# First layer's projections with both halves of h streamed past each weight, and eight modulation slabs moved into the networks

## The reference, cut to what matters

```
proj = jnp.einsum("bsd,dn->bsn", h, w_in)
q, k, v, f_logit, g_b, g_c, hc, gate_conv, gate_attn = jnp.split(proj, _SPLITS, axis=-1)
ya = g_b * causal_depthwise_conv(g_c * hc, conv_w)
yb = forgetting_attention(q, k, v, logf)
merged = sigmoid(gate_conv) * (ya @ w_branch[0]) + sigmoid(gate_attn) * (yb @ w_branch[1])
m = merged @ w_out
...
mod = c_act @ ada_w[i] + ada_b[i]      # second block, layers 0 and 1
h = rms_norm(x, norm_g[i, 0]) * (1.0 + sc_a) + sh_a
```

## Time and profile before

| | us |
|---|---|
| median of 3 runs | 962.9 (962.7 to 963.29) |
| the profiled execution | 962.54, its span 961.2 |
| TensorE busy | 953.2 (99% of the span) |
| VectorE busy | 740.0 (77%) |
| ScalarE busy | 544.8 (57%) |
| GpSimd busy | 34.2 (4%) |
| HBM read | 223.49 MB, mean 234 GB/s over the span |

### The profile page before, as it was taken

One profiled execution on the slowest core, in us unless ns is written; L12 is line 12 of the kernel. 1 busy time (PEld: TensorE's weight loads), 2 busy tenths in 40 slices (PEclk: granted clock), 3 DMA queues, 4 the chain that ended last, 5 costly groups with the idle time before them and its releaser, 6 DMA issues.

```text
span 961.2 us, 13438 instructions
## 1 busy us (share of the span) xinstructions
PE 953.2 (99%) x5418; PEld 827.7 (86%) x5418; DVE 740.0 (77%) x1145; ACT 544.8 (57%) x838; POOL 34.2 (4%) x58
## 2 busy tenths in 40 slices
PE   9999999999999999999999999999999999999997
PEld 7999989888888888888888888888888888888886
DVE  7799978788877767988678878766897678766563
ACT  6745553565455656665565454656776675454551
POOL 2000000020000001000000000001000100000000
PEclk9999999999999999999999999999999999999999
DMA  9877788498777753776467677763743266668511
GB/s 366 335 276 263 262 308 313 173 200 343 269 295 300 286 204 135 270 269 264 185 248 296 247 293 271 270 250 137 241 138 125 88 243 239 219 184 320 176 44 45
DMA packets 33151, 225.64 MB, mean 235 GB/s; under 512 B 4058, under 2 KB 4341, under 8 KB 6720
## 3 DMA queue, kind: packets, MB, share of 16 engines
q1 hardware_dynamic: 30960, 219.43, 61.8%
q0 software_dynamic: 1696, 5.08, 2.0%
q10 hardware_dynamic: 432, 0.26, 0.1%
HBM read 223.49 MB, written 1.26 MB: 234 GB/s over the span
## 4 chain that ended last, share of the span: by engine, by line
PE 93%; DVE 2%; DMA 2%; ACT 2%; SPq 0%; POOL 0%; issue 0%; DVEq 0%
PE psum L623 30%; PE psum L628 16%; PE psum L668 10%; PE psum L669 10%; PE psum L670 10%; PE psum L585 3%; PE psum L586 3%; PE psum L587 3%; DMA raw<-in_qk 2%; PE psum L888 2%; PE psum L740 1%; PE psum L739 1%; PE psum L741 1%; PE psum L320 1%; PE psum L956 1%; PE psum L601 0%
## 5 line engine op out<-in xcount | busy, mean ns | idle before, releaser
L512 DVE TENSOR_TENSOR low<-raw,high 128x2048 fp32r<-128x2048 f32 (+1 forms) x160 | 361.1, 2275 | 95.1 <-ACT high L506 95.0
L506 ACT ACTIVATE high<-raw 128x2048 fp32r<-128x2048 f32 (+1 forms) x160 | 299.9, 1897 | 15.1 <-DMA raw<-in_moba_qk 4.8
L623 PE MATMUL psum<-h_both,high 128*128 128x512 f32 x1272 | 305.3, 392 | 0.0
L623 PEld LDWEIGHTS psum<-h_both,high 128*128 128x128 f32 x1272 | 235.5, 188 | 48.2 <-issue 1.5
L628 PEld LDWEIGHTS psum<-h_both,low 128*128 128x128 f32 x1312 | 168.3, 191 | 6.4
L628 PE MATMUL psum<-h_both,low 128*128 128x256 f32 x1312 | 170.2, 283 | 0.0
L668 PE MATMUL psum<-high,y_hi 128*128 128x512 f32 x328 | 129.3, 394 | 0.0
L669 PE MATMUL psum<-low,y_hi 128*128 128x512 f32 x328 | 128.1, 391 | 0.0
L670 PE MATMUL psum<-high,y_lo 128*128 128x512 f32 x328 | 127.8, 390 | 0.0
L635 ACT ACTIVATE work_v<-psum 128x256 f32<-128x256 f32 x120 | 45.6, 383 | 142.2 <-PE psum L628 142.2
L521 DVE CUSTOM_DVE_ANT_0 raw<-raw,c_row 128x1024 f32<-128x1024 f32 x96 | 113.4, 1219 | 0.0
(11 more groups left out here) (195 smaller groups left out, 1033.6 us busy)
## 6 DMA issues: line engine op xcount, KB each, us to landing
raw<-in_gate_up SPq DMA_DIRECT2D x66, 1024.0 KB, 5.5
raw<-in_ada SPq DMA_DIRECT2D x48, 1024.0 KB, 4.9
raw<-in_down SPq DMA_DIRECT2D x33, 1024.0 KB, 4.9
raw<-in_mix SPq DMA_DIRECT2D x14, 1024.0 KB, 6.9
raw<-in_moba_qk SPq DMA_DIRECT2D x8, 1024.0 KB, 5.2
raw<-in_diff_qk SPq DMA_DIRECT2D x8, 1024.0 KB, 4.9
raw<-in_qk SPq DMA_DIRECT2D x4, 1024.0 KB, 16.2
raw<-in_branch SPq DMA_DIRECT2D x4, 1024.0 KB, 6.3
```

Source lines behind the costliest of these rows:

```text
L506: nc.scalar.activation(high[n % N_HI][:, s], raw[i % N_RAW][:, s], ACT.Copy).then_inc(*rounded.up(n if key is None else key))
L512: nc.vector.tensor_tensor(low[i % N_RAW][:, s], raw[i % N_RAW][:, s], high[n % N_HI][:, s].bitcast(F32), ALU.subtract).then_inc(*rest.up(key))
L623: nc.tensor.matmul(o[:, :], a, h_both[:, k, :, :], start=k == 0, stop=False)
```

## The change

All twelve `pe_still` slabs of the projections become `pe_both`, the first query slab in banks 5 and 6. Their results leave PSUM by `act_low` and `dve_low` where one instruction did before, and the first scores wait for the joined queries and keys. `gate_folded` goes. The second slab of the values is rounded and split in two halves. `plan` has 6, 17, 8, 13, 4 modulation slabs in its stretches where it had 14, 11, 8, 11, 4. The first transposes for the MoBA layer stand a few matmuls later in the last down slabs. GpSimd waits for x to be scaled before three of its gain transfers.

```diff
@@ -92,8 +92,8 @@
 def load_order():
 
     nets = [(NUM["gate_up1", 0], NUM["moba_v", 0]), (NUM["gate_up2", 0], NUM["diff_v", 0]), (NUM["gate_up2", 2 * FG], len(MAIN))]
-    plan = [(14, 4, 22), (11, nets[0][0] + 4, nets[0][0] + 24), (8, nets[0][1] + 4, nets[1][0] - 2),
-            (11, nets[1][0] + 3, nets[1][0] + 26), (4, nets[2][0] + 4, nets[2][0] + 16)]
+    plan = [(6, 4, 22), (17, nets[0][0] + 2, nets[0][0] + 29), (8, nets[0][1] + 4, nets[1][0] - 2),
+            (13, nets[1][0] + 2, nets[1][0] + 28), (4, nets[2][0] + 4, nets[2][0] + 16)]
     after, n = {}, 0
     for count, lo, hi in plan:
         for k in range(count):
@@ -654,13 +654,15 @@
                 (_, k0, blocks), n = parts[i], parts_n[i]
                 if i not in seen:
                     seen.add(i)
-                    yield from pe.wait_ge(rest, n)
+                    yield from pe.wait_ge(rest, (1, "a") if n == 1 else n)
                 wh = high[n % N_HI][:, :].rearrange("p (k n) -> p k n", k=kcs)
                 wl = low[SLOT[n]][:, :].rearrange("p (k n) -> p k n", k=kcs)
                 b, j = 4 + 2 * t + c, blocks.index(c)
                 if k0 == 0:
                     yield from bank((name, t, c), *freed(t, c), at=b)
                 for k in range(kcs):
+                    if n == 1 and k == kcs // 2:
+                        yield from pe.wait_ge(rest, n)
                     for signal, key in ready(k0 + k, t):
                         yield from pe.wait_ge(signal, key)
                     first, last = k0 + k == 0, k0 + k == k_all - 1
@@ -782,7 +784,8 @@
                 yield from pe_both(gate_up, base * 2 * FG + FG + g, h_ready(before), [("up", f)] if g == FG - 1 else [])
                 if g < FG - 2:
                     yield from pe_down(f, g - 1)
-            turn = {(1, 0, 1): lambda: pe_turn(behind, 0)} if behind != 5 else {}
+            hook = (1, 1, 1, 0) if behind == 1 else (1, 0, 1)
+            turn = {hook: lambda: pe_turn(behind, 0)} if behind != 5 else {}
             yield from pe_down(f, FG - 3, FG - 2, FG - 1, between=turn)
 
         def act_ffn(f):
@@ -999,8 +1002,7 @@
             for h in (n, n + 1) if n % 2 == 0 and n < H else ():
                 part = slice((h % 2) * HD1, (h % 2 + 1) * HD1)
                 sums = slice((h % 2) * HD1, (h % 2) * HD1 + CK_ROWS)
-                yield from pe.wait_ge(evacuated, ("q1", h // 4))
-                yield from pe.wait_ge(produced, ("k1", h // 4))
+                yield from pe.wait_ge(joined, ("qk1", h // 4, h // 2 % 2), ("qk1", 2 + h // 4, h // 2 % 2))
                 yield from pe.wait_ge(small_dve, "ck")
 
                 def minus_c(o, w):
@@ -1215,7 +1212,7 @@
 
             def qk(g, keys):
-                yield from pe_still("qk1", 2 * keys + g, h_of, ready, [[(produced, ("k1", g)) if keys else (evacuated, ("q1", g))]])
+                yield from pe_both("qk1", 2 * keys + g, ready, at=(None, None) if keys else (5, 6))
 
             yield from qk(0, 0)
             yield from qk(0, 1)
@@ -1235,19 +1232,16 @@
             yield from qk(1, 1)
             yield from pe_attend1(1)
             for g in range(2):
-                yield from pe_still("mix", 2 + g, h_of, ready, [[(evacuated, ("zc", g))]])
+                yield from pe_both("mix", 2 + g, ready, at=(5, 6))
                 yield from pe_attend1(2 * g + 2)
-                yield from pe_still("mix", 4 + g, h_of, ready, [[(produced, ("z", g))]])
+                yield from pe_both("mix", 4 + g, ready)
                 yield from pe_attend1(2 * g + 3)
             for g in range(2):
-                yield from pe_still("mix", g, h_of, ready, [[(produced, ("conv", g))]])
+                yield from pe_both("mix", g, ready, at=(None, None) if g else (4, 6))
                 yield from pe_attend1(6 + g)
             for n in range(2):
                 for g in range(4):
-                    if gate_folded(n, g):
-                        yield from pe_both("mix", 6 + 4 * n + g, ready, at=((4, 5) if g % 2 == 0 else (6, 7) if n else (None, None)))
-                    else:
-                        yield from pe_still("mix", 6 + 4 * n + g, h_of, ready, [[(evacuated, ("gate", n, g))]])
+                    yield from pe_both("mix", 6 + 4 * n + g, ready, at=((4, 5) if g % 2 == 0 else (6, 7) if n else (None, None)))
                     if n == 0 and g < 3:
                         yield from pe_attend1(H + g)
             conv_of = (lambda k: y_hi[:, AC + k, :], lambda k: y_lo[:, AC + k, :])
@@ -1335,6 +1329,9 @@
                 yield from act_affine("in", 1, g)
+            for i, kind, m in act.items(1):
+                yield from act_round(1, 1, slice(0, SLAB // 2), (1, "a"))
+                yield from act_round(1, 1, slice(SLAB // 2, SLAB))
             yield from act_split(AHEAD)
             yield from act_next("v1", 1)
             yield from act_values("v1", 0)
@@ -1352,27 +1349,28 @@
 
             def query(g):
                 yield from act_next("qk1", g)
-                yield from act.wait_ge(slab, ("qk1", g))
                 yield from act.wait_ge(h_lo_made, ("in", 1, KC - 1))
-                nc.scalar.activation(qT[:, 2 * g:2 * g + 2, :], pair(bank_of["qk1", g, 0]), ACT.Copy, scale=HD1 ** -0.5).then_inc(
-                    *evacuated.up(("q1", g)))
+                yield from act_low(("qk1", g), qT[:, 2 * g:2 * g + 2, :], HD1 ** -0.5)
+
+            def key(g):
+                yield from act_next("qk1", 2 + g)
+                yield from act_low(("qk1", 2 + g), kT[:, 2 * g:2 * g + 2, :])
 
             yield from query(0)
-            yield from act_next("qk1", 2)
+            yield from key(0)
             yield from act.wait_ge(small_dve, "cq")
             nc.scalar.activation(pick[:, :], col("pick"), ACT.Copy)
             nc.scalar.activation(ck[:, :], psum[bank_of["sums"]][:, S:2 * S], ACT.Copy).then_inc(*small_act.up("ck"))
             yield from query(1)
             yield from act_attend1(0)
-            yield from act_next("qk1", 3)
+            yield from key(1)
...
@@ -1389,15 +1389,11 @@
                     yield from act_next("mix", index)
                     two = slice(2 * g, 2 * g + 2)
-                    yield from act.wait_ge(lo_made, ("conv", 1))
-                    if gate_folded(n, g):
-                        yield from act_low(("mix", index), place[:, two, :])
-                        yield from act.wait_ge(joined, ("mix", index, 1))
-                        src = place[:, two, :]
-                    else:
-                        yield from act.wait_ge(slab, ("mix", index))
-                        src = pair(bank_of["mix", index, 0])
-                    nc.scalar.activation(place[:, two, :], src, ACT.Sigmoid).then_inc(*evacuated.up(("gate", n, g)))
+                    if n == 1:
+                        yield from act.wait_ge(lo_made, ("conv", 1))
+                    yield from act_low(("mix", index), place[:, two, :])
+                    yield from act.wait_ge(joined, ("mix", index, 1))
+                    nc.scalar.activation(place[:, two, :], place[:, two, :], ACT.Sigmoid).then_inc(*evacuated.up(("gate", n, g)))
                     if n == 0 and g < 3:
                         yield from act_attend1(H + g)
@@ -1539,10 +1538,10 @@
             def key(g):
                 yield from dve_next("qk1", 2 + g)
-                yield from dve.wait_ge(slab, ("qk1", 2 + g))
-                nc.vector.tensor_copy(kT[:, 2 * g:2 * g + 2, :], pair(bank_of["qk1", 2 + g, 0])).then_inc(*produced.up(("k1", g)))
+                yield from dve_low(("qk1", 2 + g), kT[:, 2 * g:2 * g + 2, :])
 
             yield from dve_next("qk1", 0)
+            yield from dve_low(("qk1", 0), qT[:, 0:2, :], HD1 ** -0.5)
             yield from key(0)
             yield from dve.wait_ge(small_pe, "sums")
             nc.vector.tensor_copy(c_q[:, :], psum[bank_of["sums"]][:, 0:NT * H]).then_inc(*small_dve.up("cq"))
@@ -1552,18 +1551,19 @@
             m.then_inc(*small_dve.up("ck"))
             yield from dve_next("qk1", 1)
+            yield from dve_low(("qk1", 1), qT[:, 2:4, :], HD1 ** -0.5)
             yield from dve_attend1(0)
             yield from key(1)
             yield from dve_attend1(1)
             for g in range(2):
                 two = slice(2 * g, 2 * g + 2)
                 yield from dve_next("mix", 2 + g)
+                yield from dve_low(("mix", 2 + g), zc[:, two, :])
                 yield from dve_attend1(2 * g + 2)
                 yield from dve_next("mix", 4 + g)
...
@@ -1696,13 +1695,16 @@
             yield from pool_spread()
             yield from pool_gain(0, 0, None)
             yield from pool_post_norm(1)
+            yield from pool.wait_ge(scaled, (1, NT - 1, 1))
             yield from pool_gain(0, 1, 0)
             yield from pool_post_norm(2)
             yield from pool_post_norm(3)
+            yield from pool.wait_ge(scaled, (3, NT - 1, 1))
             yield from pool_gain(1, 0, 1)
             for h in range(0, H, 2):
```

(1 more changed line is left out.)

28 lines of the change are left out of this document (14 added, 14 removed).

## The result

The changed kernel takes **972.5 us** (median of 5 runs, 969.87 to 973.18) against 962.9 (962.7 to 963.29) before: 1.0091, 95% interval [1.008, 1.0103]. It is slower by 9.6 us, and the forecast of 963.1 with its range up to 965.9 misses it. The profiled execution took 973.18 us, its span 971.9.

A forecast was written before the change was run, and what follows sets the result against it. TensorE, busy 953.2 of 961.2 us, was taken as the bound. +3.25 (new wait) - 2.2 (faster slabs) - 0.42 (`ck` stall gone) - 0.4 (GpSimd) = +0.2 on the profiled 962.54, a median of 963.1 us; range 961.5 to 965.9.

The forecast's parts named there:

- Eight slabs in the networks, at nothing: Modulation slabs moved into the networks cost nothing; VectorE goes from 82% to 86% in the first; lost cover at most 2.4 us.
- The clock falls in the hole: Rival: TensorE's 3.2 us idle before the first query slab lowers the clock, 1.1 to 3.0 us, middle 2.0, 965.1; chance 0.32.
- The new wait: First query slab waits for ScalarE to copy bank 5, starting at 29.12 instead of 25.87 us: +3.25 us, bounds 2.6 to 3.5.
- The faster slabs: Twelve projection slabs on TensorE take 5.57 instead of 5.755 us each, with 16 fewer instructions: -2.2 us.
- Two-bank evacuation, at nothing: Extra copies and additions, at most 10 us of VectorE, covered by eight departing modulation slabs, 19 us; uncovered, 0.4 to 2.5 us.
- GpSimd and the turn: After the first two networks, gain transfers no longer run beside the scaling of x: 0.21 us each, -0.4 us; MoBA turn's move nothing.

The follow-up runs named there:

- plan_only: The kernel before with the new plan numbers (6, 17, 8, 13, 4) and nothing else: 968.73 us, ratio 1.0058.
- mid10: bank7 with 10, 13, 8, 13, 4 modulation slabs: 961.92 us, ratio 0.9986 to the kernel before.
- half_sum: bank7 with all slabs and transfers, but VectorE sums only 512 of every 1024 columns of slabs 6 to 22: 962.43 us, ratio 0.9991.
- filled_hole: The changed kernel with 17 small products on TensorE ahead of the first query slab, the wait staying: 971.51 us, ratio 1.0085.
- bank7: The changed kernel with its first query slab in banks 7 and 6 instead of 5 and 6: 966.32 us, ratio 1.0031.
- hook10: mid10 with the first transposes for the MoBA layer and GpSimd's waits for scaled x as before the change: 961.55 us, ratio 0.9978.
- bank7_old_plan: bank7 with the plan of before (14, 11, 8, 11, 4): 968.82 us, ratio 1.0059.
- net15: bank7 with 8, 15, 8, 13, 4 modulation slabs, the first network's behind +3 to +24: 970.25 us, ratio 1.0069.
- moba10: bank7 with 8, 13, 10, 13, 4 modulation slabs: 968.0 us, ratio 1.0048.
- early17: bank7 with the first network's 17 slabs behind +2 to +24, not +29, and the second's 13 up to +24, not +28: 966.32 us, ratio 1.0034.

## Why the prediction was wrong

**"Eight slabs in the networks, at nothing" is the step that failed**, with 5.6 of the 6.2 us lost in the first network: 4.1 us of waits, which plan_only shows without any other edit, and 1.5 of fallen clock behind them. It took VectorE's 82%, and 86% with the new slabs, as a sign of room. Of the idle time, 34.4 us in the first network, nearly all was waiting for ScalarE in a chain in which ScalarE waited for VectorE, and only some of it could be filled: two more slabs (mid10), not six. It also bounded the lost cover by "at most one modulation slab, 2.4 us" at a wait for `low`; the waits were for `y_lo`, 2.7, and for a join, 0.9, and it had no price for the clock behind them. half_sum shows that most of it is VectorE's time, 4.0 of 5.6 us; the rest is open, with the transfers as the likely part.

**"The clock falls in the hole"** was a rival with 0.32 and the middle price of 2.0; it happened at 2.95, near its upper price of 3.0, so the forecast took the wrong side, and these us are missing from its sum. The Trainium skill (TensorE: Matmul & The Clock Gate, Why this matters for your kernels) warns of an idle gap between bursts, and the trace of after agrees, with its 4.66 us and the clock at 0.50.

**"The new wait"** was right in its chain and short in its size: 4.05 us instead of 3.25. All of the difference is that slab 4 landed at 24.15 and not 23.35, which differs from execution to execution; in filled_hole it landed at 23.39 and the slab started at 29.16, 0.04 us off the forecast. bank7 shows wait and clock together: 6.2 us by one line of banks.

**"The faster slabs", -2.2**, hold: each changed slab brings TensorE 0.17 to 0.18 us forward in the new trace, 3.0 us in bank7 by 105 us with the `ck` wait (0.42) in it.

**"Two-bank evacuation, at nothing"** was true only because eight slabs left at the same time. With the old plan in place it costs 10 us between 12 us (0.0) and the end of the first layer (+7.0, where bank7 has -3.2). I had the trade, 10 us against 19, but not that the old density was already at the limit; VectorE is 19.72 of 20 us busy there in the earlier trace rows.

**"GpSimd and the turn", -0.4**, came, and was lost again beside it. The second turn takes 1.06 us behind the first network and 1.07 behind the second where it took 1.27 at both before, 0.2 us each; in hook10, where the transfer again leaves beside the scaling (666.57), the turn behind the second network takes 1.27 again. The distance from turn to turn behind the second network fell by 0.35 more (669.50 to 678.78 is 9.28 us, 658.59 to 668.22 was 9.63); hook10 keeps that (658.00 to 667.29), so it isn't GpSimd's order. Every kernel here with the new projections has it and none with the old; what gives it is open. Against these stand 0.28 us of waiting behind the third network and the turn for the MoBA layer. The forecast moved that one by three matmuls and put it at "Nothing", because it asked only when the values want the turned h. Its own second turn comes 9.24 us behind the first wherever the first stands, so the move cost 0.55 us (mid10 against hook10), with a wait of 0.72 for the scaled x.

**The sum** from its measured parts: first layer 4.05 + 2.95 - 3.0 = 4.0 (seen: 4.3), network 4.1 + 1.5 + 0.6 = 6.2, later +0.2, together 10.4 on the profiled 962.54, 972.9 (seen: 973.18, 10.6 more). The profiled execution is the slowest of the five; the medians are 9.6 apart.

## What to carry to other kernels

An engine's busy share is no measure of its room: look at whom it waits for in its idle time. Where that is an engine that in turn waits for it, as for nearly all of VectorE's 34.4 idle us of 167 here, only part of the time can be filled, and the sum of work and waits doesn't say how much: it reached the whole stretch with 11 and with 13 slabs, at no loss, and with 17, at 4.1 us. So when a transfer or sum is moved out of a full stretch, try the number that moves as a parameter; here plans with 6 to 14 slabs in the first layer, the rest elsewhere, span 961.5 to 970 us with the banks put right, while the faster matmul form, with the best plan on both sides, is worth 0.1 to 0.5 us, which the runs don't tell from nothing. A wait of TensorE of some 2.6 us or more should be priced with a possible fall of the clock behind it; the waits of 1.3 to 1.8 us here had none.

## What the runs showed of the hardware

The granted clock fell to 0.50 behind a wait of 4.66 us (at 30 us, for some 6 us, 2.95 us lost) and behind waits of 2.64 to 3.51 us in bank7_old_plan, bank7, the changed kernel, filled_hole, net15 and moba10. It did not fall behind the same wait of 2.70 us in plan_only and early17, whose next products ran at full rate:
```profile
362.00:364.00 2.00, 0.31 (x1) 0.30 (x2) 0.85 (x2) 1.81 (x2) 0.00 (x0) 1.00 0.00 0
364.00:366.00 2.00, 2.00 (x10) 1.66 (x9) 1.34 (x1) 1.21 (x3) 0.00 (x0) 1.00 0.00 0
```
(stretches of early17, columns as above). So at this length the wait alone doesn't decide. What does stays open, and with it some 1.5 us of any forecast at such a hole.
